# Seven block products for a fourth k-tile pair of the attention gate columns

## What is computed

```python
u = rmsnorm(h, mix_pre_g[l])
proj = u @ w_in[l]
q, k, v, qi, ki, wi, glu_in, gates = jnp.split(proj, IN_OFFSETS, axis=-1)
attn = dsa_attention(q, k, v, qi, ki, wi, rel_bias) @ w_o[l]
conv = conv_module(glu_in, conv_dw[l], conv_dw_b[l], conv_ln_g[l],
                   conv_ln_b[l], w_pw2[l])
g_attn, g_conv = jnp.split(jax.nn.sigmoid(gates + b_gate[l]), 2, axis=-1)
mixed = (g_attn * attn + g_conv * conv) @ w_out[l]
h = h + rmsnorm(mixed, mix_post_g[l])
```

## Time and profile before

| | |
|---|---|
| median of 3 runs | 2056.43 us (2056.26 to 2056.82) |
| profiled execution | 2056.37 us, of which the span of the trace is 2054.7 us |
| PE busy | 2044.1 us, 99% of the span |
| DVE busy | 1800.5 us, 88% |
| ACT busy | 1175.6 us, 57% |
| matmuls in the trace | 9220 |

### The profile page before, as it was taken

The page is one execution under the profiler, slowest core; times in us unless marked ns, Lnnn a source line. Parts: engine busy times, 40 slices in busy tenths (PEclk is TensorE's granted clock), DMA queues, the critical chain, the costliest instruction groups (busy, mean ns, idle before and its releaser), DMA issues.

```text
span 2054.7 us, 26436 instructions
## 1 busy us (share of the span) xinstructions
PE 2044.1 (99%) x9220; PEld 1692.1 (82%) x9220; DVE 1800.5 (88%) x2089; ACT 1175.6 (57%) x1305; POOL 97.2 (5%) x134
## 2 busy tenths in 40 slices
PE   9999999999999999999999999999999999999998
PEld 8888888888888788888788888888888888888886
DVE  7999899989888858998687998878999899999897
ACT  6565665657555554444466555565656566665563
POOL 0010001000000000100000000000000000000000
PEclk9999999999999999999999999999999999999999
DMA  9787777865656666776555566567778777846564
GB/s 333 231 234 228 223 216 235 243 206 183 197 195 205 190 186 193 205 206 185 171 169 183 176 194 226 189 232 236 216 236 240 211 225 230 235 148 210 195 205 164
DMA packets 223518, 430.49 MB, mean 210 GB/s; under 512 B 16394, under 2 KB 16658, under 8 KB 223041
## 3 DMA queue, kind: packets, MB, share of 16 engines
q1 hardware_dynamic: 209904, 401.26, 60.5%
q0 software_dynamic: 13376, 27.98, 7.4%
q10 hardware_dynamic: 144, 0.04, 0.0%
HBM read 427.12 MB, written 2.11 MB: 209 GB/s over the span
## 4 chain that ended last, share of the span: by engine, by line
PE 98%; DVE 1%; issue 0%; ACT 0%; POOL 0%; DVEq 0%; POOLq 0%; ACTq 0%
PE banks L1966 97%; PE banks L2017 2%; DVE res L1212 0%; DVE act_lo L1225 0%; ACT act_hi L620 0%; DVE wlo L1157 0%; DVE comb L1181 0%; POOL stat L504 0%; ACT junk L687 0%; PE banks L2264 0%; PE banks L2265 0%; PE banks L2266 0%; DVEq L125 0%; PE banks L2218 0%; PE banks L2234 0%
## 5 line engine op out<-in xcount | busy, mean ns | idle before, releaser
L605 ACT ACTIVATE whi<-raw 128x1024 fp32r<-128x1024 f32 x579 | 598.6, 1052 | 410.2 <-PE banks L1966 298.6
L1157 DVE TENSOR_TENSOR wlo<-raw,whi 128x1024 fp32r<-128x1024 f32 x580 | 688.7, 1215 | 104.2 <-ACT whi L605 101.6
L1966 PE MATMUL banks<-whi,act_hi 128*128 128x512 f32 x1532 | 497.4, 395 | 0.0
L1966 PE MATMUL banks<-whi,act_lo 128*128 128x512 f32 x1532 | 488.2, 389 | 0.0
L1966 PE MATMUL banks<-wlo,act_hi 128*128 128x512 f32 x1532 | 472.1, 389 | 0.0
L1966 PEld LDWEIGHTS banks<-wlo,act_hi 128*128 128x128 f32 x1532 | 287.5, 188 | 60.5 <-DVE wlo L1157 0.2
L1966 PEld LDWEIGHTS banks<-whi,act_lo 128*128 128x128 f32 x1532 | 287.6, 188 | 60.2
L1966 PEld LDWEIGHTS banks<-whi,act_hi 128*128 128x128 f32 x1532 | 284.7, 188 | 59.8 <-issue 3.4
L605 ACT ACTIVATE whi<-raw_deep 128x1024 fp32r<-128x1024 f32 x176 | 183.4, 1056 | 73.4 <-PE banks L1966 70.9
L1157 DVE TENSOR_TENSOR wlo<-raw_deep,whi 128x1024 fp32r<-128x1024 f32 x176 | 207.6, 1219 | 7.0 <-ACT whi L605 6.9
L739 ACT ACTIVATE wsum_hi<-wsum 128x1536 fp32r<-128x1536 f32 x80 | 119.0, 1487 | 150.2 <-PE banks L1966 87.0
(11 more groups left out here) (339 smaller groups left out, 2460.0 us busy)
## 6 DMA issues: line engine op xcount, KB each, us to landing
raw<-in_ffn_wd_dram SPq DMA_DIRECT2D x176, 512.0 KB, 4.8
raw<-in_w_in_dram SPq DMA_DIRECT2D x160, 512.0 KB, 3.6
raw<-in_ffn_wg_dram SPq DMA_DIRECT2D x88, 512.0 KB, 4.3
raw_deep<-in_ffn_wg_dram SPq DMA_DIRECT2D x88, 512.0 KB, 4.1
raw<-in_ffn_wu_dram SPq DMA_DIRECT2D x88, 512.0 KB, 5.1
raw_deep<-in_ffn_wu_dram SPq DMA_DIRECT2D x88, 512.0 KB, 5.3
raw<-in_w_out_dram SPq DMA_DIRECT2D x32, 512.0 KB, 4.6
raw<-in_ffn_wu_dram POOLq DMA_DIRECT2D x40, 256.0 KB, 5.3
```

The source lines that it names most:

```text
L605: nc.scalar.activation(whi[:, j % RING, 0:kts * width], src[:, 0:kts * width], ACT.Copy).then_inc(hi_ready, 1)
L1157: nc.vector.tensor_tensor(wlo[:, j % RING, 0:n], raw_slot(j, deep)[0][:, 0:n], whi[:, j % RING, 0:n], ALU.subtract).then_inc(lo_ready, 1)
L1966: return nc.tensor.matmul(o, a, b, **kw)
```

## The change

Pair 4 joins `GATE_SEVEN`: four of the eight pairs are made with seven block products, the fourth to the seventh in a row (q = 3, 4, 5, 6), in both pairs of chunks. The activation sums are now four sets and are made earlier in the lists of DVE and ACT: the second low half and the third set in pair 2, the third low half and the fourth set in pair 3, the fourth low half in pair 4. To have room, the activation sums move over the attention's tensors (`o_q` and on) and the sums for the product with `w_out` over the convolution's input. Nothing else is touched. The weight sums of pair 4 follow from `GATE_SEVEN` by the code as it was.

```diff
-GATE_SEVEN = (3, 5, 6)
+GATE_SEVEN = (3, 4, 5, 6)
...
-        gsum_hi, _ = sb("gsum_hi", [P, len(GATE_SEVEN), 4, P], f32r, over=o_cin)
-        gsum_lo, o_glo = sb("gsum_lo", [P, len(GATE_SEVEN), 4, P], f32r, over=o_cin + SUM * len(GATE_SEVEN))
+        gsum_hi, _ = sb("gsum_hi", [P, len(GATE_SEVEN), 4, P], f32r, over=o_q + KT * SEQ * 2)
+        gsum_lo, o_glo = sb("gsum_lo", [P, len(GATE_SEVEN), 4, P], f32r, over=o_q + KT * SEQ * 6)
...
-        out_at = [o_glo + SUM * len(GATE_SEVEN), o_q + 2 * KT * SEQ * 4, o_cin, o_cin + 2 * SUM]
-        assert out_at[0] + 2 * SUM <= o_qi and out_at[1] + 2 * SUM <= o_bias + 4 * HEADS * SPAN
+        out_at = [o_cin + 2 * SUM * k for k in range(len(OUT_SEVEN))]
+        assert out_at[-1] + 2 * SUM <= o_qi and SUM * len(GATE_SEVEN) <= KT * SEQ * 2
...
-                    if p == 0 and q == 4:
-                        gate_sums_hi(1)
                     if q in GATE_SEVEN:
                         act.wait_ge(wsum_ready, 4 * seven + 1)
                     hi_in(name, 2 * q + 1)
                     if p == 0 and q < 3:
                         attend(7 + q)
-                    if p == 0 and q == 4:
-                        gate_sums_hi(2)
+                    if p == 0 and q in (2, 3, 4):
+                        gate_sums_hi(q - 1)
...
+                    if p == 0 and q == 2:
+                        gate_sums_lo(1)
+                        gate_sums(2)
                     if p == 0 and q == 3:
-                        gate_sums(2)
+                        gate_sums_lo(2)
+                        gate_sums(3)
                     if p == 0 and q == 4:
-                        gate_sums_lo(1)
-                        gate_sums_lo(2)
+                        gate_sums_lo(3)
```

## The result

The changed kernel takes 2065.03 us, the median of 6 runs (2064.92 to 2065.7), the kernel before 2056.46 (6 runs, 2056.26 to 2056.91). The ratio is 1.004, with a 95% interval of 1.003 to 1.005: slower by 8.6 us, where the prediction had 8.2.

A forecast was written before the change was run, and what follows sets the result against it. PE (99% busy) bounds the kernel, with DVE a second bound in the gate pairs, hidden by a small lead. Waits of 5.66 and 3.93 less 1.36 for matmuls give +8.23 on 2056.37: 2064.6 us, range 2060.4 to 2067.0.

The forecast's parts named there:

- Fewer matmuls: Pair 4, once in each pair of chunks, goes from 24 to 21 matmuls: 1.36 us less on PE.
- DVE's lag as the bound: Gate pairs: DVE needs 6.71 us per seven-product pair, 1.95 more than PE, losing that much lead in every further pair.
- The five waits: PE waits 1.28, 2.43, 1.95 us at pairs 4, 5, 6 of the first chunks; 1.98, 1.95 at 5, 6 of the second.
- the walk: Both gate stretches, stepped through from the earlier trace's DVE and PE timelines: waits of 5.66 and 3.93 us.
- The 0.2 for PE's restart: Behind each PE wait for `wlo`: one weight load, 0.2 us, taken between bounds of 0 and 0.4.
- What is hidden: Gate stretches: ACT's added copies and SP's later loads stay covered, and the moved buffers cost 0.
- The rival of no waits: DVE's new gate-pair work stays beside PE, so only 1.36 us goes: 2055.0 us; chance 0.08.
- From 5.7 us more DVE lead no wait is left: Entry to pair 3, first pair of chunks: the lead at which the rival of no waits would hold; 3.9 in the second.
- The rival that the second pair of chunks keeps up: Waits there shrink to nothing if ACT's copy comes earlier: +4.3 us, 2060.7; chance 0.12.
- the ring: Single buffers `wsum`, `wsum_hi`, `gate_wsum_lo` tying DVE, ACT, PE; forecast used `wsum_hi` for pair 5's 1.98 wait, second chunks.
- The clock: Rival: waits in the gate pairs drop PE to 1.2 GHz; once adds 4.8 us, 2069.4; chance 0.05.
- The base: Whole kernel before the change: profiled execution of 2056.37 us, to which the forecast added 8.23.

## Why the prediction was right, point by point

*Fewer matmuls.* Six fewer are in the trace, and the pairs without waits take 4.76. The 1.36 us are there.

*DVE's lag as the bound.* Right. The round of 6.72 against 4.76 is the 1.95 per pair of the prediction. Shorter rounds (5.25) took the waits away, an operation more lengthened the waits by its own time where the clock stayed, and in the kernel before the lead took most of the same operation.

*The five waits.* All five are within 0.02 us of the walk, the second pair of chunks included, with one idle of DVE of 0.99 (predicted about 1.1) before the low half of pair 4. The 0.2 for PE's restart was a choice between 0 and 0.4 that no row showed; that it fits is luck. It is made of the low passes' 0.73 in place of 0.61 and the rest ahead of the first of them. It also weighs less than the prediction said, which let the restarts of all five waits add up to about 1 each way. In a row that DVE paces, a pair that ends later shortens the next wait by as much, so by the prediction's own walk 0.2 more or less counts once in each pair of chunks, 0.4 in all.

*What is hidden.* No gap of PE was released by a DMA or by ACT in these stretches. Moved buffers and order: 0, as taken (minus 0.15 measured).

*The rival of no waits.* Its time was rightly rejected, but the point from which it was to decide was wrong. "From 5.7 us more DVE lead no wait is left" reckons with totals, as if DVE could run ahead without end. With 6.7 us less work for DVE, 4.4 of the 5.7 stayed. The lead at pair 3 grew by 2.1 only in that run, but DVE stood idle before the low half of pair 4, so more of it could not be used. A lead lasts as far as the next single buffer: the low half of a pair can't start before PE has ended the pair before. The prediction had used that very wait in the second pair of chunks, but not for this figure.

*The rival that the second pair of chunks keeps up.* Its totals, 43.2 against 42.3, almost did; but the run with pair 4 there alone still waits 1.69 and 1.67 by the timeline. Without the ring (second `wsum_hi`) the first of these is 0.61, the second stays.

*The clock.* It did not fall in the profile of the changed kernel (1.00 in both stretches). Its mechanism exists, though, and its price was sized wrongly: not a pair at half rate, 4.8 us, but windows of four microseconds at 0.57 to 0.60, worth 1.6 at the end of a row and nothing within one, where DVE sets the pace. The rule that the prediction set beside it (the Trainium skill, "TensorE: Matmul & The Clock Gate", section "HAM oscillation — how this bites in real kernels") is borne out in kind by the runs with the falls, and not by the changed kernel's own trace, where five pauses of 0.98 to 2.15 us brought none.

*The base.* 8.29 by the pairs, 8.57 by the medians. The 0.3 between them is less than the 0.8 between the fastest and the slowest run of the changed kernel; no row explains it.

## What to carry to other kernels

Before an engine at 99% is relieved, take the stretch in which the edit lies and set the next engine's round against its own: here 6.7 us of VectorE for each 4.8 of TensorE, hidden only by a lead of a few microseconds that a longer row of such pairs uses up. Walk such a row instruction by instruction from the trace of before, with the lead at the entry and the buffer that each step waits for; totals tell that there will be waits, the walk tells how long. A lead is worth only what the single buffers let the engine run ahead, so removing work in front of the row (1.3 us gained here) buys little without a second buffer, and a second buffer (1.2) little without less work for the engine; both together gave 4.0, and 1.47 us less work in each round alone gave 7.2.

## What was not expected of the hardware

*TensorE's clock behind short waits.* It fell to the 1.2 GHz level behind waits of 2.73 and 2.25 us (the run with one operation more) and of 2.10 (second `wsum_hi`); it stayed at 1.00 behind 2.29 in the first of these runs, 2.15 in the changed kernel and 2.16 in the run without activation sums. So the length of the one wait doesn't decide it, and the runs here don't show what does. Nor did the fall come at one place: in the first case it began while PE still stood in the wait, in the other two about a microsecond after PE had gone on. By windows of one microsecond each slow stretch was between three and four long, at a granted clock of 0.50.

*GpSimd beside VectorE.* Equal operations of VectorE took 2.12 in place of 1.23 and up to 1.96 in place of 1.22, while GpSimd made sums; moving 7.1 us of work off VectorE brought it only 0.8 us ahead at the sums of pair 4 (1154.84 against 1156.39, in a trace that runs 0.74 earlier).
